# Silu by tanh and sigmoid by exponential in the mixers, decays in nine wider-spaced steps, the attention branch's norm in another bank, and the last pair squared first at the stages' ends

## The reference

```python
# first block
h = rms_norm(x, norm_mix_g) * (1 + sc_m) + sh_m
a_q, a_k, a_v, b_q, b_ff, b_fb, b_i, b_g, c_q, c_k, c_v, c_g, c_lrf, c_lrb, gates = split(h @ w_in)
q_b   = silu(b_q) * 64 ** -0.5                     # branch b, 4 heads of 64
log_f = log_sigmoid(z) + log1p(lb * exp(min(-z, 80)))   # z: b_ff or b_fb, lb: a lower bound per feature
k_b   = (1 - lb) * sigmoid(-z)
o_b   = rms_norm(bidir_scan(q_b, k_b..., b_i, log_f...)) * silu(b_g)
o_c   = rms_norm(bidir_scan(c_q * 32 ** -0.5, c_k, c_v, log_a...)) * silu(c_g)
o_a   = rms_norm(softmax(q1 k1) v - lam * softmax(q2 k2) v) * 0.8    # branch a, 4 heads
merged = g_a * (o_a @ w_up_a) + g_b * (o_b @ w_up_b) + g_c * (o_c @ w_up_c)   # g = sigmoid(gates)
x = x + gt_m * (merged @ w_out)
h = rms_norm(x, norm_mlp_g) * (1 + sc_f) + sh_f
x = rms_norm(x + gt_f * (relu(h @ mlp_w1) ** 2 @ mlp_w2), final_norm_g)
# second block, two layers
x = x + rms_norm(mixer(rms_norm(x)))     # layer 0: sliding window attention; layer 1: chunked SGU
x = x + rms_norm(ffn(rms_norm(x)))       # gelu(conv(g)) * u, then down
```

## Time and profile before

| | |
|---|---|
| median of 3 runs | 2381.29 us (2379.55 to 2382.61) |
| profiled execution, its own time | 2383.91 us |
| its span in the trace | 2382.2 us |
| TensorE's granted clock, mean over the span | 0.983 |
| PE busy (matmuls) | 2285.8 us, 96% |
| PEld busy (weight loads, beside PE) | 1905.5 us, 80% |
| DVE, ACT, POOL busy | 1143.4, 1016.9, 1053.1 us |

### The profile page before, as it was taken

How to read it: one execution, slowest core, us unless ns; L and a number is a source line. 1 busy time by engine, 2 the same in 40 slices (tenths; PEclk the granted TensorE clock), 3 DMA queues, 4 the chain that set the end, 5 groups by cost and what they waited for, 6 DMA issues and landing times. The chain is left out here.

```text
span 2382.2 us, 28986 instructions
## 1 busy us (share of the span) xinstructions
PE 2285.8 (96%) x11624; PEld 1905.5 (80%) x11624; DVE 1143.4 (48%) x1746; ACT 1016.9 (43%) x1897; POOL 1053.1 (44%) x804
## 2 busy tenths in 40 slices
PE   7989988999999999999999999999999999999998
PEld 4768766777888888888888888878888888888887
DVE  3666877755441122457475244451343345724253
ACT  4675566644443232555553222363332235422224
POOL 1444333343544454632435444534444443544454
PEclk9989999999999999999999999999999999999999
DMA  7221232356222322321212222323222222222321
GB/s 280 80 71 71 107 120 93 133 177 239 89 80 97 106 89 91 109 76 36 89 54 106 89 90 105 106 71 106 89 89 89 90 87 72 95 100 86 109 90 70
DMA packets 42663, 239.80 MB, mean 101 GB/s; under 512 B 5024, under 2 KB 7072, under 8 KB 17184
## 3 DMA queue, kind: packets, MB, share of 16 engines
q1 hardware_dynamic: 39328, 231.23, 27.2%
q10 hardware_dynamic: 3200, 6.71, 1.0%
HBM read 226.38 MB, written 8.39 MB: 99 GB/s over the span
## 5 line engine op out<-in xcount | busy, mean ns | idle before, releaser
L2571 POOL TENSOR_TENSOR WL<-RAW,WH 128x512 fp32r<-128x512 f32 (+1 forms) x692 | 913.5, 1349 | 1173.3 <-ACT WH L1277 1162.0
L723 PE MATMUL PS<-HHI,WH 128*128 128x512 f32 x1496 | 601.3, 402 | 2.2 <-DVE HLO L1855 1.6
L723 PE MATMUL PS<-HHI,WL 128*128 128x512 f32 x1496 | 585.8, 392 | 0.0
L723 PE MATMUL PS<-HLO,WH 128*128 128x512 f32 x1496 | 585.6, 391 | 0.0
L1277 ACT ACTIVATE WH<-RAW 128x512 fp32r<-128x512 f32 (+1 forms) x692 | 379.9, 612 | 403.7 <-PE PS L723 382.3
L723 PEld LDWEIGHTS PS<-HHI,WH 128*128 128x128 f32 x1496 | 283.0, 189 | 75.8 <-issue 13.8
L723 PEld LDWEIGHTS PS<-HHI,WL 128*128 128x128 f32 x1496 | 282.5, 189 | 60.7
L723 PEld LDWEIGHTS PS<-HLO,WH 128*128 128x128 f32 x1496 | 283.3, 189 | 57.2 <-issue 2.2
L723 PE MATMUL PS<-UF,WH 128*128 128x512 f32 (+1 forms) x832 | 225.7, 359 | 0.0
L1855 DVE TENSOR_TENSOR T<-PS,R 128x512 f32<-128x512 f32 x112 | 76.9, 690 | 212.4 <-PE PS L723 204.4
L723 PEld LDWEIGHTS PS<-UF,WH 128*128 128x128 f32 x832 | 149.8, 191 | 22.8
(11 more groups left out here) (352 smaller groups left out, 3611.1 us busy)
## 6 DMA issues: line engine op xcount, KB each, us to landing
RAW<-in_wts SPq DMA_DIRECT2D x190, 1024.0 KB, 4.8
FW<-in_wts SPq DMA_DIRECT2D x6, 1024.0 KB, 17.3
spill<-T SPq DMA_DIRECT2D x24, 256.0 KB, 3.3
RAW<-in_wts SPq DMA_DIRECT2D x8, 768.0 KB, 4.1
GT<-spill SPq DMA_DIRECT2D x20, 256.0 KB, 4.8
X<-in_xt SPq DMA_DIRECT2D x2, 1024.0 KB, 9.2
out_x<-X SPq DMA_DIRECT2D x8, 256.0 KB, 2.2
X<-in_xt SPq DMA_DIRECT2D x2, 768.0 KB, 9.4
```

The lines of the kernel that those rows point to most:

```text
L723: return e.matmul(o_, l, r, start=start, stop=stop)
L2571: return e.tensor_tensor(o_, a, b, f)
```

## The change

It has three parts.

At the stages' ends, ACT squares the last pair of half 0 before it splits b: of b's splits two follow the square and two come between the high parts of the next stage's blocks 0 to 2. The adds of pairs 1 and 2 of half 0 move from GpSimd to VectorE, one place behind the takes of the next pair. The squares of half 0, and that of pair 3 of half 1, go to bank 6 of PSUM instead of SBUF. GpSimd does the low parts of a and b without a break and then the two adds of half 1. Squares of pairs 2 and 3 of half 0 wait for the add of the pair before.

In the mixers' first part, `silu(z)` is made as z times (tanh(z/2) + 1), with the factor 1/2 put elsewhere: ACT's evict of cg, bg and bq writes Tanh of half the PSUM tile; one row later a new step `silu` has VectorE do (t + 1) * z with z read from PSUM; for bq the scale becomes 0.0625, and for b and c the branch norm's Exp has a bias of -ln 2 from a third column of EPSC. The bank is in use one row longer. The four DMA issues of bq go to a step `copies`, one more row later. `sigmoid(-z)` is made as exp(-(max(z, 0) + ln(1 + exp(-|z|)))): the logarithm is there already for the log decay, VectorE adds the maximum to it in one pass over 1024 columns, a pass that was not there before, and ACT's Exp stands behind the others. The decays have nine steps instead of seven, begin at rows 16 and 34 with gaps of 2 and 2.2, do one running sum per step, and scale the key last.

The mean of the attention branch's norm goes to bank 0 instead of bank 1.

```diff
 NATURAL = ("cv", "bv", "av")
-GATE_C, DECAY, RECUR, ATTEND = (1, 2), ((19, 1.5), (30, 1.5)), (9, 1.1), (75, 1.7)
+GATE_C, DECAY, RECUR, ATTEND = (1, 2), ((16, 2), (34, 2.2)), (9, 1.1), (75, 1.7)
...
-        late = []
+        late, later, copies = [], [], []
...
                     step = [("nat", i, m, row // 2)] * (row % 2 == 0) if natural else [("gemm", i, m, 2 * row)]
-                    yield step + beside[r] + (late if row == 1 else [])
+                    yield step + beside[r] + (late if row == 1 else []) + (later if row == 2 else []) + (copies if row == 3 else [])
                 late = [("evict", i, tag, n, m)]
+                later = [("silu", i, tag, m)] if tag in ("cg", "bg", "bq") else []
+                copies = [("copies", m)] if tag == "bq" else []
...
     def decays(self, p):
-        for n in range(7):
+        for n in range(9):
...
     LB = place("LB", o, [24]); o += 96
-    EPSC = place("EPSC", o, [2]); o += 32
+    EPSC = place("EPSC", o, [3]); o += 32
...
         if kind == "a":
-            return 2, 1, 128, ones, SC[:, 3:4], None, (OA[:, n, 0, :], OA[:, n, 1, :]), T0[1][:, :], SS[:, :]
+            return 2, 0, 128, ones, SC[:, 3:4], None, (OA[:, n, 0, :], OA[:, n, 1, :]), T0[1][:, :], SS[:, :]
...
-    def square_of(p):
-
-        return SS if p == 0 else SQ if p == 2 else T0[0]
+    def square_of(hf, p):
+        return SS[:, :] if p == 0 else PS[:, 6, :] if hf == 0 or p == 3 else SQ[:, :] if p == 2 else T0[0][:, :]
...
                     q.wait_ge(*at(("sum", n, 0)))
-                elif p == 2 and hf:
-                    q.wait_ge(*at(("ssa", n, 0, 2)))
-                elif p == 3:
-                    q.wait_ge(*at(("ssa", n, hf, 1)))
-                elif p == 1 and hf:
-                    q.wait_ge(*at(("ssa", n, 0, 3)))
-                dst = square_of(p)[:, :].rearrange("p (k t) -> p k t", k=2)
+                elif p > 1 and hf == 0:
+                    q.wait_ge(*at(("ssa", n, 0, p - 1)))
+                dst = square_of(hf, p).rearrange("p (k t) -> p k t", k=2)
...
             squares(0, 2)
-            for p in range(4):
-                split(b, p)
...
             squares(0, 3)
+            for p in range(2):
+                split(b, p)
...
                 high(0, k)
-                if 4 + k < 5:
-                    split(b, 4 + k - 1)
+                if k < 3:
+                    split(b, 1 + k)
...
             TA, TB, TC = [g_[:, :, :] for g_ in G3]
-            if n == 0:
+            if n == 1:
                 q.wait_ge(*at(("ev", U["bz", p], 1)))
-                e.activation(K_, Z, ACT.Sigmoid, scale=-1.0).then_inc(*up("a_mix", ("sg", p)))
-            elif n == 1:
...
                 e.activation(TC, TC, ACT.Exp, scale=-1.0).then_inc(*up("a_mix", ("ec", p)))
+                q.wait_ge(*at(("lk", p)))
+                e.activation(K_, K_, ACT.Exp, scale=-1.0).then_inc(*up("a_mix", ("sg", p)))
...
                 q.wait_ge(*at(("ln", kind, n)))
-                e.activation(rr, rr, ACT.Exp, scale=-0.5).then_inc(*up("a_mix", ("r", kind, n)))
+                half_ = {} if kind == "a" else {"bias": EPSC[:, 2:3]}
+                e.activation(rr, rr, ACT.Exp, scale=-0.5, **half_).then_inc(*up("a_mix", ("r", kind, n)))
...
                 q.wait_ge(*at(("t", i, m)))
-            if tag == "cg":
-                e.activation(GC[:, m, :], ps, ACT.Silu).then_inc(*up("a_ev", ("ev", i, m)))
+            if tag in ("cg", "bg"):
+                e.activation((GC if tag == "cg" else GB)[:, m, :], ps, ACT.Tanh, scale=0.5).then_inc(*up("a_ev", ("tanh", i, m)))
...
                 q.wait_ge(*at(("h", "mix", 6 + m)))
-                e.activation(tm[:, :], ps, ACT.Silu).then_inc(*up("a_ev", ("ev", i, m)))
-                q.wait_ge(*at(("q_scaled", m)))
-                for k in range(4):
-                    h2, d = k // 2, k % 2
-                    t = e.dma_start(keyed(2 * m + h2)[64 * d:64 * d + 64, 0, :], tm[64 * h2:64 * h2 + 64, :])
-                    t.then_inc(*up(f"dupq{m}", *([("qb", m)] if k == 3 else []), by=16))
-            elif tag == "bg":
-                e.activation(GB[:, m, :], ps, ACT.Silu).then_inc(*up("a_ev", ("ev", i, m)))
+                e.activation(tm[:, :], ps, ACT.Tanh, scale=0.5).then_inc(*up("a_ev", ("tanh", i, m)))
...
+        def copies(m):
+            q.wait_ge(*at(("q_scaled", m)))
+            for k in range(4):
+                h2, d = k // 2, k % 2
+                t = e.dma_start(keyed(2 * m + h2)[64 * d:64 * d + 64, 0, :], T0[2 + m][64 * h2:64 * h2 + 64, :])
+                t.then_inc(*up(f"dupq{m}", *([("qb", m)] if k == 3 else []), by=16))
...
                 evict(*a)
+            elif step == "copies":
+                copies(*a)
...
                 q.wait_ge(*at(("ssa", n, hf, p - 1) if p > 1 else ("sqp", n, hf, 0)))
-                tt(SS[:, :], SS[:, :], square_of(p)[:, :], ADD).then_inc(*up("d_norm", ("ssa", n, hf, p), *([("ssh", n, hf)] if p == 3 else [])))
+                tt(SS[:, :], SS[:, :], square_of(hf, p), ADD).then_inc(*up("d_norm", ("ssa", n, hf, p), *([("ssh", n, hf)] if p == 3 else [])))
...
                 take(0, p)
+                if p > 1:
+                    add(0, p - 1)
...
         e.memset(EPSC[:, 0:1], EPS)
+        e.memset(EPSC[:, 2:3], -math.log(2.0))
...
         def decay(p, n):
-            Z = ZB[:, 2 * p:2 * p + 2, :]
+            Z, K_ = ZB[:, 2 * p:2 * p + 2, :], QKB[:, 2 - 2 * p:4 - 2 * p, 1, :]
             TA, TB, TC = [g_[:, :, :] for g_ in G3]
-            if n == 1:
-                q.wait_ge(*at(("sg", p)))
-                q.wait_ge(*at(("lb", 5)))
-                for h in (2 * p, 2 * p + 1):
-                    ts(keyed(h)[:, 1, :], keyed(h)[:, 1, :], LB[:, 16 + h:17 + h], None, MUL).then_inc(*up("d_mix", ("kb", h)))
-            elif n == 2:
+            if n == 2:
...
                 q.wait_ge(*at(("la", p)))
+                stt(K_, Z, 0.0, TA, MAX, ADD).then_inc(*up("d_mix", ("lk", p)))
+                q.wait_ge(*at(("lk", p)))
...
                 q.wait_ge(*at(("log_b", p)))
-                scans(ZB, (2 * p, 2 * p + 1), "decay_b")
+                scans(ZB, (2 * p,), "decay_b")
+            elif n == 7:
+                q.wait_ge(*at(("log_b", p)))
+                scans(ZB, (2 * p + 1,), "decay_b")
+            elif n == 8:
+                q.wait_ge(*at(("sg", p)))
+                q.wait_ge(*at(("lb", 5)))
+                for h in (2 * p, 2 * p + 1):
+                    ts(keyed(h)[:, 1, :], keyed(h)[:, 1, :], LB[:, 16 + h:17 + h], None, MUL).then_inc(*up("d_mix", ("kb", h)))
...
                 e.tensor_copy(VC[:, 2 * m:2 * m + 2, :], ps.rearrange("p (t n) -> p t n", t=2)).then_inc(*up("d_ev", ("ev", i, m), ("vc", m)))
-            elif tag == "bq":
-                q.wait_ge(*at(("ev", i, m)))
-                ts(T0[2 + m][:, :], T0[2 + m][:, :], 0.125, None, MUL).then_inc(*up("d_mix", ("q_scaled", m)))
...
+        def silu(i, tag, m):
+            a = T0[2 + m][:, :] if tag == "bq" else (GC if tag == "cg" else GB)[:, m, :]
+            q.wait_ge(*at(("tanh", i, m)))
+            stt(a, a, 1.0, PS[:, BANK[i, m], :], ADD, MUL).then_inc(*up("d_ev", ("ev", i, m)))
+            if tag == "bq":
+                q.wait_ge(*at(("ev", i, m)))
+                ts(a, a, 0.0625, None, MUL).then_inc(*up("d_mix", ("q_scaled", m)))
...
                 evict(*a)
+            elif step == "silu":
+                silu(*a)
...
-            def add(hf, p):
-                q.wait_ge(*at(("sqp", n, hf, p)))
-                q.wait_ge(*at(("ssa", n, hf, p - 1) if p > 1 else ("sqp", n, hf, 0)))
-                tt(SS[:, :], SS[:, :], square_of(p)[:, :], ADD).then_inc(*up("p_norm", ("ssa", n, hf, p)))
+            def add(p):
+                q.wait_ge(*at(("sqp", n, 1, p)))
+                q.wait_ge(*at(("ssa", n, 1, p - 1) if p > 1 else ("sqp", n, 1, 0)))
+                tt(SS[:, :], SS[:, :], square_of(1, p), ADD).then_inc(*up("p_norm", ("ssa", n, 1, p)))
...
             if nx is None:
-                add(0, 1)
-                add(0, 2)
...
                 return
-            split(a, 0)
-            split(a, 1)
-            add(0, 1)
-            split(a, 2)
-            split(a, 3)
-            add(0, 2)
-            for p in range(4):
-                split(b, p)
-            add(1, 1)
-            for p in range(4, 4):
-                split(b, p)
-            add(1, 2)
+            for u in (a, b):
+                for p in range(4):
+                    split(u, p)
+            add(1)
+            add(2)
```

More of the change, by code:

```diff
@@ L1 @@
+import math
 import concourse.bass as bass
```

## The result

The changed kernel took 2352.67 us, the median of 4 runs (2349.91 to 2359.09), beside 2381.77 us of the kernel before in the same comparison: a ratio of 0.9883, 95% interval 0.986 to 0.9906, so 22 to 33 us less; the two medians differ by 29.1 us. A second comparison, further down, gave 2352.19 and 0.9863 (0.9841 to 0.9885). The forecast was 2346.1 with a range of 2328 to 2366. The profiled execution of the changed kernel took 2350.67 us, its span 2348.8 (granted clock 0.992, before 0.983): 33.4 us less span, where the sum of the prediction's terms was 35.2.

What follows compares the result with a forecast made beforehand. TensorE, busy 96% of the span, was taken as the bound, so only its waits and low clock could give time. Ends 19.6, mixers' halves 7.5 and 8.1 sum to 35.2 us, giving a median of 2346.1 us, range 2328 to 2366.

Steps and rivals of the forecast that it cites:

- Ends: Stages' ends: waits for the sums of squares and their clock loss go, less new HLO waits; 19.6 us gained, bounds 10 to 27.
- The milder of the two cases: Behind the ends' sums: low parts held for one GpSimd instruction, blocks 3 and 4 coming 2.1 and 0.3 us late.
- The hold: SGU's end: GpSimd's splits hold VectorE's add, 3.86 us instead of 0.69; with a PSUM operand it takes about 0.7.
- First half of the mixers: Decays and Silu: waits of 6.40 and 2.67 us shrink or go, with clock loss; 7.5 us gained, bounds -3 and 16.
- the charge of 1.5: Mixers, 165 to 215 us: cost in us charged for about 12 us more VectorE work there, bounds 0 and 12.
- Tanh: Mixers' evicts of cg, bg and bq on ACT: Tanh needs 0 table loads, standing among Exps.
- Rival 4: Mixers: Tanh loads tables as Silu does; about 6 us less gain, 2352 us; chance 0.03.
- Second half: Mixers' attention norms: transposes no longer wait for the norm, bg's Silu loads go; 8.1 us gained, bounds 2 and 14.
- The signs: Expected traces: no SS waits at four ends, adds 0.7 us, HLO waits 3 to 4 us, no Tanh loads.
- (1): Stages' ends give half back, new waits being long enough to lower the clock: 2356 us; chance 0.17.
- (2): Mixers give nothing, VectorE gets more work and the stalls only change place: 2362 us; chance 0.15.
- (5): Mixers, 165 to 215 us: VectorE becomes the bound and the clock falls; slower, +13 us, 2395; chance 0.04.

Runs made afterwards that it cites:

- e5_sbuf_squares: The changed kernel, but with the squares of half 0 in SBUF again instead of PSUM bank 6: 2354.16 us, ratio 0.9898 to the kernel before.
- e6_last_square_psum: The kernel before, with only the last square of half 0 (pair 3) in PSUM bank 6 at the first four ends: 2368.24 us, ratio 0.9958.
- e4_silu: The kernel before, with only Silu replaced by Tanh and a product on VectorE, decays and bank unchanged: 2374.54 us, ratio 0.9967.

## Why the prediction was right, point by point

**The bound.** It was TensorE's waits and its clock, as forecast: 22.3 and 11.1 us of 33.4.

**Ends, 19.6 forecast, 19.8 in the trace, 20.2 timed.** The terms were 5.9, 5.9, 5.3, 2.9 and -0.4 for the first feed-forward, the SGU, the mixers, the attention and the last end; the two profiles give 5.5, 5.4, 6.35, 2.65 and -0.1. The arrival of square and add was right: 0.9 and 0.2 us ahead of TensorE were forecast, 0.8 and 0.05 came. The HLO waits behind the sum were taken at 3.6 us new against 2.0 old. At the attention's and the SGU's end they are 2.04 against 0.8, at the first feed-forward's 0.77 against none, and at the mixers' 1.03 where 2.2 was forecast. Taken together with these, an old long wait with its clock cost 6.3 to 7.4 us, where 7.5 was taken, and the attention's 3.9 instead of 4.5. So both sides of the term were too large, and that they nearly cancelled is partly luck. A part of the excess is in the working itself: 21 matmuls of 0.12 us are 2.5 us, so the four us at 0.51 lost 1.5 and not 1.7. The milder of the two cases came, low parts held by no more than one GpSimd instruction (1.31 and 0.84 for 0.48). One piece was missed: the add of pair 3, held by no port but by a plain wait for GpSimd's add, cost the larger share, 1.37.

**That the term came out rests on the execution it was read from.** Against the four executions with the old ends, everything behind the first sum is 19.8, 11.5, 21.9 and 19.4 us shorter in the changed kernel, 18.2 in the mean. A range for the old waits themselves was missing in the working; against the second of the four the same forecast would have been 8 us too high.

**The hold.** That GpSimd's burst stretches a two-operand add in SBUF, and that an operand in PSUM frees it, is shown: 0.98 to 3.98 us in one case, 0.69 in all four in the other. The Trainium skill (SBUF — State Buffer, on who interferes with whom) says that a VectorE instruction with at most one SBUF input, outside the modes in which it uses two ports, doesn't contend with GpSimd; by that rule, the trace agrees. By an estimate from these rows, one GpSimd instruction of 1.24 us would stretch the add to 0.69 + 1.24 = 1.93 us at most. That fits the adds of 0.98 to 1.51 and the low parts shown, and not the adds of 2.57 to 3.98. But the prediction let the reader think that both causes went with the change; e5_sbuf_squares shows that the earlier square is enough, and e6_last_square_psum that PSUM alone gives half of it by the times and three quarters by the traces.

**First half of the mixers, 7.5 forecast, 5.3 by the two profiles, 5.9 by the means.** One cost was taken too small: the new pass of VectorE was taken at 1.8 us, and the first took 3.42 (the second 1.21). It has two operands in SBUF; it began at 104.98 beside a GpSimd instruction and ended 1.1 us after that one (107.31). It stands right ahead of the collect, so a wait of 2.27 us came at 110, where 0.31 and 1.24 had been. The 6.40 us wait became 3.46, "near 3" as forecast. But the sum had used 4.6 us for it, which would leave 1.8: counted from the first product, this wait ended 94.8 us on instead of 97.2, 2.4 earlier, and the pass explains 1.6 of the 2.2 that are missing. In 165 to 215 VectorE was busy 41.1 of 50 us instead of 31.3 and TensorE 49.6: the charge of 1.5 was enough.

**Tanh.** Five of the six Tanhs load nothing; the one at 152.18 loads, since a Ln of the second decay with a load of its own stands before it at 146.89. ACT's loads up to 620 us are 32 instead of 42. The Trainium skill (ScalarE: Activation LUTs, Table sets) lists tanh in Exp's set, and by that rule, the trace agrees. Rival 4 is out.

**Second half, 8.1 forecast, 7.55 by the profiles, 6.3 by the means; its shares were wrong.** The working gave the bank all but 2.6 us of 8.8 and took 0.7 off for the longer hold. The runs give the bank about 2 (265.0 to 262.8 alone, 262.9 to 258.7 at most in the whole) and Silu 4 or more (e4_silu alone: 258.2, one execution). Two things failed, and that the sum came out near is luck: the collect behind the norm wasn't what held the product, bank 2 was, and that is emptied by the same norm; and ACT's loads for bg stood ahead of the norm itself, so that without them the first such wait falls from 4.87 to 2.04 with the bank unchanged.

**The signs.** The waits for SS, the windows behind them and the adds of 0.69 us came as forecast; one Tanh of six loads. The HLO waits were 0.8 to 2.0 us an end and not 3 to 4. One sign of being wrong came: SCT waits above 15 us in all were to mean an error, and they are 16.9 (16.0 in the second profile of the changed kernel). In the first half they fell from 10.6 to 6.2 us as meant, but in the second they rose from 8.4 to 10.7: where the norm had held TensorE, the collects now do in part. At the third norm, for one, waits of 0.86 for ACT and 1.91 for SCT became one of 2.96 for SCT. The working had no such term.

**Rivals.** (1) and (2) didn't come; the medians (2352.7 and 2352.2) lie between the forecast's own value and them largely because the profiled execution of before was 2.1 above its median and that of after 2.0 below: 33.4 of span are 29.1 of median. (5) asked for VectorE as the bound from 165 to 215; its busy share there rose, but TensorE lost 0.45 us.

**Open.** The second half is 261.9 to 267.7 us long in four executions with the same norms and Silu, and their waits agree to 1 us. The rest lies in the granted clock (0.98 from 250 to 505 us in the shortest of them, 0.95 in the longest), and no run here says what decides it. Why decays and Silu give more together than apart is open too.

## What to carry to other kernels

Ask of a late operand first when it was made and only then who holds it: the earlier square made the holder harmless. Where two engines share adds of one sum, look for the plain wait of one for the other's slower add, and put it behind the work that others need. And look at a wait in several executions before its size goes into a sum: if it comes in steps of another engine's instruction, one profile shows one draw.

## What was not expected of the hardware

VectorE's add got in among GpSimd's four splits (1.24 us each) at different places in different executions of the same code. In four executions with the old ends, 16 cases, it ended about 3.05, 4.3 or 5.5 us after the burst began, so that it took 0.98 to 1.51, 2.57 to 2.95 or 3.49 to 3.98 us. When it got in before the last split, the burst took about 5.4 us instead of 4.95. Two parts that gave 0.2 and 1.7 us alone gave 5.9 together.
